# Handing over from one row phase to the next in a two-layer PEER trunk: tokens spread inside the last run, sum read behind the first groups, groups dealt anew

## What is computed

```python
def one_block(xb):                       # 128 tokens
    q = (xb @ w_q).reshape(128, 8, 2, 128)
    s = einsum('tphd,phnd->tphn', q, subkeys)
    s1, i1 = top_k(s[:, :, 0], 16);  s2, i2 = top_k(s[:, :, 1], 16)
    cand = s1[..., :, None] + s2[..., None, :]
    top, pos = top_k(cand, 16)           # 16 experts for each of 8 heads
    g = softmax(top)
    act = gelu(einsum('tped,td->tpe', u[eidx], xb))
    return einsum('tpe,tped->td', g * act, v[eidx])
```

## Time and profile before

| | us |
|---|---|
| runs: median of 3 | 2404.1 (2401.18 to 2404.43) |
| the profiled execution's own time | 2406.2 |
| its span, first to last instruction | 2404.4 |
| mean granted TensorE clock | 0.817 of full |

### The profile page before, as it was taken

One profiled execution on the slowest core, in us unless ns is written; L12 is line 12 of the kernel. 1 busy time (PEld: TensorE's weight loads), 2 busy tenths in 40 slices (PEclk: granted clock), 3 DMA queues, 4 the chain that ended last, 5 costly groups with the idle time before them and its releaser, 6 DMA issues. The chain is left out here.

```text
span 2404.4 us, 28976 instructions
## 1 busy us (share of the span) xinstructions
PE 1595.4 (66%) x9342; PEld 841.6 (35%) x9342; DVE 1567.5 (65%) x4320; ACT 845.8 (35%) x2751; POOL 843.6 (35%) x772
## 2 busy tenths in 40 slices
PE   8986876895965454666764586877577445655554
PEld 6774543563632111333431263545253101200010
DVE  2456787655567778555689558765675897665654
ACT  2324344532323323443333435543232234322232
POOL 0012333432343333243433424343425444444341
PEclk9998897897978777887886898788788677777777
DMA  9978899999899999999999999999999999999996
GB/s 387 408 250 346 326 404 411 397 419 410 345 419 419 420 420 419 396 401 420 414 418 396 419 418 400 371 406 419 417 367 420 422 421 422 421 421 421 422 422 258
DMA packets 156955, 956.48 MB, mean 398 GB/s; under 512 B 19076, under 2 KB 21764, under 8 KB 58500
## 3 DMA queue, kind: packets, MB, share of 16 engines
q0 software_dynamic: 110592, 805.36, 81.2%
q1 hardware_dynamic: 40880, 144.94, 15.6%
q10 hardware_dynamic: 5332, 4.33, 0.7%
HBM read 951.67 MB, written 2.89 MB: 397 GB/s over the span
## 5 line engine op out<-in xcount | busy, mean ns | idle before, releaser
L774 POOL DMA_INDIRECT rows<-in_uv,eidx x768 | 843.4, 1098 | 1516.8 <-PE acc L857 1124.5
L1382 DVE CUSTOM_DVE_ANT_0 rows<-rows,xrep 128x1024 f32<-128x1024 f32 x768 | 911.9, 1222 | 398.2 <-DMA rows<-in_uv,eidx 363.7
L857 PE MATMUL acc<-rows,diag 128*32 128x512 f32 x3072 | 776.8, 751 | 550.3 <-ACT diag L1081 529.1
L857 PEld LDWEIGHTS acc<-rows,diag 128*32 128x32 f32 x3072 | 155.2, 127 | 1072.5 <-ACT diag L1081 701.9
L1081 ACT ACTIVATE act_out<-act_in 128x2 f32<-128x2 f32 x384 | 77.8, 203 | 920.3 <-DVE act_in L1382 886.5
L1081 ACT ACT_TABLE_LOAD x121 | 155.2, 1283 | 232.1 <-DVE act_in L1382 140.7
L792 PE MATMUL bank<-wt,hT 128*128 128x256 f32 x888 | 202.9, 388 | 18.8 <-ACT hT L1081 6.7
L1081 ACT ACTIVATE diag<-small,wv 128x32 f32<-128x32 f32 x768 | 204.9, 314 | 12.5
L792 PEld LDWEIGHTS bank<-wt,hT 128*128 128x128 f32 x888 | 170.3, 194 | 60.2 <-issue 15.7
L1081 ACT ACTIVATE wv<-act_out,gate 128x1 f32<-128x1 f32 x768 | 184.3, 287 | 12.6
L792 PE MATMUL bank<-hT,wt 128*128 128x256 f32 (+1 forms) x896 | 174.0, 356 | 8.4 <-ACT hT L1081 7.9
(11 more groups left out here) (174 smaller groups left out, 1435.0 us busy)
## 6 DMA issues: line engine op xcount, KB each, us to landing
wt<-in_ada_w SPq DMA_DIRECT2D x60, 512.0 KB
wt<-in_peer_w_q SPq DMA_DIRECT2D x48, 512.0 KB
rows<-in_ada_w SPq DMA_DIRECT2D x36, 512.0 KB, 15.2
wt<-in_mlstm_w_in SPq DMA_DIRECT2D x27, 512.0 KB
rows<-in_uv,eidx POOLq DMA_INDIRECT x768
wt<-in_attn_w_qkv SPq DMA_DIRECT2D x24, 512.0 KB
rows<-in_mlstm_w_in SPq DMA_DIRECT2D x21, 512.0 KB, 15.9
rows<-in_peer_w_q SPq DMA_DIRECT2D x16, 512.0 KB, 11.6
```

The costliest lines, as they stand in the source:

```text
L774: nc.gpsimd.indirect_dma_start(out=rows[:, r, :], out_offset=None, in_=A["uv"], in_offset=bass.IndirectOffsetOnAxis(ap=eidx[:, b, slot:slo ...
L857: last = nc.tensor.matmul(acc[c:c + QUAD, h * 512:(h + 1) * 512], diag[:, r, :], rows[:, r, D + h * 512:D + (h + 1) * 512], start=first, s ...
L1382: last = V.tensor_tensor_reduce(out=rows[:, r, 0:D], in0=rows[:, r, 0:D], in1=xrep[:, GS * odd + j, :], scale=1.0, scalar=0.0, op0=ALU.mul ...
```

## The change

1. XR becomes two plan steps, one for each half (slabs 0 and 1, slabs 2 and 3), four PSUM tiles each. Both stand behind GATE, ahead of the phase's last run.
2. On PE half 0 is filled at that place; half 1 is filled behind the last run's groups, before the last owed sums are paid.
3. ACT copies half 0 just ahead of the phase's group 63, when 63 of the 64 groups have had their dot products, and half 1 behind group 63's own work.
4. FIN moves behind the next phase's first groups: 2 in phase two, 1 in phases three and four, 2 in five and six. The load of the cached keys and values (CACHE) goes along with FIN.
5. Phase one's last three groups now follow GATE.
6. DEALS and PATIENCE of phases two, three and four are new. The table shows the groups of the phase that stand ahead of some steps, before and after:

| step | before | after |
|---|---|---|
| phase two: PQ first | 0 | 2 |
| phase two: PQ second, third | 2, 11 | 4, 14 |
| phase three: NORM, NT, AQKV first | 0, 1, 3 | 1, 3, 3 |
| phase three: last PT, PC, PG, GATE | 48, 50, 50, 50 | 47, 47, 49, 49 |
| phase four: NORM, NT, NORM, NT | 0, 3, 6, 6 | 1, 2, 2, 3 |
| phase four: AQKV 1, 2, 3 | 8, 11, 13 | 3, 6, 11 |
| phase four: first and last attention head (AS to AV) | 18 to 21, 37 to 40 | 17 to 19, 39 to 42 |
| phase four: OUT 1, 2 | 44, 50 | 43, 47 |
| phase four: PT, PC, PG; GATE | 58; 61 | 59; 59 |
| phase five: PQ first | 0 | 2 |

```diff
+GORDER = [(0, 0), (0, 1), (0, 2), (1, 0), (1, 1), (1, 2)]
+AHEAD_OF_SUM = 2
...
     def spread(l, b, steps):
 
         steps = list(steps)
-        if (l, b) != (0, 0):
-            yield ("XR", l, b)
+        order = GORDER.index((l, b))
+        following = [("XR", *GORDER[order + 1], half) for half in range(2)] if order + 1 < len(GORDER) else []
+
+        def opening(ahead):
+
+            if ahead:
+                yield ("GROUPS", l, b, 0, ahead, PATIENCE.get((l, b, 0), 2))
+            if order:
+                yield ("FIN", *GORDER[order - 1])
+            if (l, b) == (1, 0):
+                yield ("CACHE",)
+
...
-            if ahead:
-                yield ("GROUPS", l, b, 0, ahead, PATIENCE.get((l, b, 0), 2))
+            yield from opening(ahead)
             for s, n in zip(steps, counts):
                 yield s
+                if s[0] == "GATE":
+                    yield from following
...
-            yield ("FIN", l, b)
             return
         total = sum(cost(s) for s in steps)
-        done = spent = 0
+        done, spent = AHEAD_OF_SUM, 0
+        yield from opening(done)
...
         yield ("GATE", l, b)
+        yield from following
         yield ("GROUPS", l, b, done, GROUPS, 2)
-        yield ("FIN", l, b)
...
             def straight(g0, g1):
                 for g in range(g0, g1):
+                    if g == GROUPS - 1:
+                        before_last()
                     n = base + g
                     body(order, n, g * GS, n % RING, n // RING, g, False, upper(order, g))
...
             if hi == GROUPS:
-                last_ones()
+                behind_last()
...
+            def spread_rows(s):
+
+                first = P * (s[2] == 2)
+                for i in range(QUADS):
+                    t = open_tile(i)
+                    at = first + QUAD * (2 * s[3] + i // 2)
+                    for q in range(4):
+                        for copy in range(QUADS):
+                            last = mm(t[quadrant(copy), q * P:(q + 1) * P], hT[:, 4 * (i % 2) + q, at:at + QUAD], ident, True, True)
+                    last.then_inc(tile_full, 1)
+
+            def close_phase(order):
+
+                if order + 1 < len(GORDER):
+                    begin(PLAN.index(("XR", *GORDER[order + 1], 1)))
+                    spread_rows(("XR", *GORDER[order + 1], 1))
+                settle(0)
...
                 if k == "GROUPS":
-                    run_groups(pe, s, group, looped, lambda: settle(0))
+                    run_groups(pe, s, group, looped, behind_last=lambda: close_phase(GORDER.index(s[1:3])))
...
+            def spread_rows(order, half):
+
+                if order < len(GORDER):
+                    if order:
+                        act.wait_ge(dots, order * GROUPS - 1 + half)
+                        begin(PLAN.index(("XR", *GORDER[order], half)))
+                    for i in range(QUADS):
+                        copy_tile(i, xrep[:, 2 * half + i // 2, 512 * (i % 2):512 * (i % 2) + 512])
...
-                    run_groups(act, s, group)
+                    following = GORDER.index(s[1:3]) + 1
+                    run_groups(act, s, group, before_last=lambda: spread_rows(following, 0), behind_last=lambda: spread_rows(following, 1))
```

More of the change, by code:

```diff
@@ L144, in spread @@
             steps.append(("GATE", l, b))
-            assert len(counts) == len(steps) and ahead + sum(counts) == GROUPS
+            assert len(counts) == len(steps) and ahead + sum(counts) == GROUPS and counts[-1] > 1
             done = ahead
-            if ahead:
-                yield ("GROUPS", l, b, 0, ahead, PATIENCE.get((l, b, 0), 2))
+            yield from opening(ahead)
             for s, n in zip(steps, counts):
                 yield s
+                if s[0] == "GATE":
+                    yield from following
                 if n:
@@ L204, in plan @@
     yield from (("NT", 0, 1, 0), *cell(["MLU"], 0), *cell(["MLU"], 1), ("STATE",))
-    yield from (("PQ", 0, "P", 0), ("PS", 0, "P", 0, 0), ("PQ", 0, "P", 1), ("XR", 0, 0))
+    yield from (("PQ", 0, "P", 0), ("PS", 0, "P", 0, 0), ("PQ", 0, "P", 1), ("XR", 0, 0, 0), ("XR", 0, 0, 1))
     yield from ((k, 0, "P", 0, 0, half) for half in range(2) for k in ("PT", "PC", "PG"))
@@ L218, in plan @@
     yield from spread(0, 2, [*attention("P"), *norm(1, 1, "P"), *choice(1, "P", 0, every, True)])
-    yield ("CACHE",)
     seen = list(attention("S"))
@@ L223, in plan @@
     yield from spread(1, 2, [*choice(1, "S", 1, range(2, QUARTERS), False), ("YOUT", 1)])
+    yield ("FIN", *GORDER[-1])
     yield ("YOUT", 2)
@@ L236, in in_order @@
 def in_order(who):
-    late = {"P": (), "A": ("NT", "MLQK", "MLV", "MLO", "AQKV", "PQ", "OUT", "T2", "PS", "MLB", "MLE", "MLN", "AS", "MR", "XR"),
+    late = {"P": (), "A": ("NT", "MLQK", "MLV", "MLO", "AQKV", "PQ", "OUT", "T2", "PS", "MLB", "MLE", "MLN", "AS", "MR"),
             "D": ("NT", "MLQK", "MLV", "MLO", "MLM", "MLN", "AQKV", "PQ", "OUT", "T2", "PS", "MLB", "MLE", "MLU", "MC", "AS", "AP", "AV")}[who]
@@ L298, in psum_tiles @@
     if k == "XR":
-        return "A" * (2 * QUADS)
+        return "A" * QUADS
     if k == "AT":
@@ L635, in begin @@
                 s = PLAN[i]
-                if s[0] in (*IDLE[who], "GROUPS") or (s[0] == "XR" and who == "A" and s[1:] != (0, 0)) \
+                if s[0] in (*IDLE[who], "GROUPS") or (s[0] == "XR" and who == "A" and s[1:3] != (0, 0)) \
                         or (s[0] == "MC" and (who == "A") != (s[1:3] == (1, 0))) \
@@ L680, in spread_out @@
             def spread_out(order, c):
-                return owner[before[PLAN.index(("XR", *GORDER[order]))][0] + 2 * c + 1][1]
+                return owner[before[PLAN.index(("XR", *GORDER[order], c // 2))][0] + 2 * (c % 2) + 1][1]
             return begin, of, tile, full, by, emptied, next_of, one, noted, spread_out
@@ L707, in upper, with run_groups @@
             return g // (QG // 2) if (order, g // QG) == (0, 0) else g % 2
-        GORDER = [(0, 0), (0, 1), (0, 2), (1, 0), (1, 1), (1, 2)]
-        def run_groups(eng, s, body, looped=lambda n: None, last_ones=lambda: None):
+        def run_groups(eng, s, body, looped=lambda n: None, before_last=lambda: None, behind_last=lambda: None):
             _, l, b, lo, hi, _ = s
@@ L728, in run_groups @@
             straight(lo + 1, g)
-            whole = (hi - g) // UNROLL
+            whole = (hi - g - (hi == GROUPS)) // UNROLL
             if whole >= 2:
@@ L1021, in _ @@
                 elif k == "XR":
[L1022 to L1029, removed]
+                    if s[3] == 0 or s[1:3] == (0, 0):
+                        spread_rows(s)
                 elif k == "AT":
@@ L1270, in _ @@
                 elif k == "XR":
-                    act.wait_ge(dots, GORDER.index(s[1:]) * GROUPS) if s[1:] != (0, 0) else None
-                    for i in range(2 * QUADS):
-                        copy_tile(i, xrep[:, i // 2, 512 * (i % 2):512 * (i % 2) + 512])
+                    if s[1:3] == (0, 0):
+                        spread_rows(0, s[3])
                 elif k == "PG":
```

2 lines of the change are left out of this document (1 added, 1 removed), and 8 rows, old and new, of the table DEALS.

## The result

The changed kernel takes 2390.9 us (median of 6, 2381.8 to 2395.3) against 2402.7 (2401.2 to 2404.4): a ratio of 0.9935, interval 0.9915 to 0.9955. The medians differ by 11.9 us, the ratio stands for 15.6 us (10.8 to 20.4). The forecast was 2388, in the range 2377 to 2402. The experiments ran on three other chips, by all that their times say, and on the one where the changed kernel itself was repeated it won 4.5 us by the medians (3.6 by the ratio, 1.0 to 6.0).

The account below looks back on a forecast made before the run. Transfers were the bound, with time won only where they pause. Handovers 13.4 us plus new deals 3, in all 16, took 2406.2 to 2390; as that execution lay 2.1 above the median, the forecast was 2388, range 2377 to 2402.

Parts of the forecast that it names:

- memory-limit rule: Whole kernel: about 358 GB/s a core from HBM, so filled pauses only slow the rest and nothing is won; chance 0.01.
- The handovers, 13.4 us: Pauses won at phases one to two 4.8 us, two to three 3.2, four to five 5.4; ends 6 and 15.4.
- Rival (b): Handovers win 13.4 us, but full stretches of phases three and four lose 9 to 13: 2400 to 2404 us; chance 0.12.
- old pauses that grow by what the handovers win: Sign of a wrong forecast: existing transfer pauses lengthen by as much as is won between phases.
- Half 0 at nothing: First half of XR on PE ahead of the last run: 4.5 to 5.3 us, hidden by outstanding transfers, so no cost.
- every half 0: By the skill's clock rule, each first half of XR would run at the lower clock, 9 to 10 us.
- 0 to 3 us for the owed sums: Phase one to two: two owed sums behind GATE and half 0 hold two gathers, pausing transfers nothing to 3 us.
- sign of being wrong: A sum delayed over 5 us behind half 0, with the DMA share dropping before the handover.
- DVE's earlier start: New phase's first dot product starts some 1 to 2 us after the last old one; DVE gains 11 to 15 us each.
- Gather 7: Phase one to two: this gather issued near 612 us in place of 624.9, ahead of the 618 when it was due.
- The new deals, 3 us: Groups dealt anew in phases three and four: between winning all 10.9 us and a loss as large, taken as 3.
- The rival of a slower phase four: Three AQKV among phase four's groups 3 to 11 at lower clock: new pause some 30 us, 2418 us; chance 0.07.

Follow-up runs that it names:

- the repeat: The kernel before, run once more without an edit on one of the three other chips: 2383.0 us, ratio 1.0001.
- the repeats: The kernel before and the changed kernel, each run again without an edit on the other chips: 2383.0 us and 2379.6 us.
- XR doubled: The changed kernel with each of XR's small matmuls issued twice: 2387.8 us, ratio 1.0009 to the kernel before.
- the undisturbed repeat: The changed kernel run again without an edit on one of the three other chips: 2379.6 us, ratio 0.9985 to the kernel before.
- before doubled: The kernel before with each of XR's small matmuls issued twice, 512 in place of 256 for each handover: 2419.3 us, ratio 1.0142.

## Why the prediction was right, and where it wasn't

**The bound** was read rightly: what was won in the first profile was, but for some 2 us, pauses filled at an unchanged 421 GB/s. The memory-limit rule of the Trainium skill that the prediction weighed (DMA: Bandwidth & Descriptors, Where 436 GB/s comes from) doesn't fit these runs: the core moved 421 GB/s for 200 us on end, and the closed pauses did shorten the time.

**The handovers, 13.4 us.** On the first chip the three windows came out at 1.00 to 1.02. The single terms: one to two won about 4.3 us of phase two's 6.8 (4.8 put; what is left is 1.1 us behind half 0 and 1.1 us at 640 to 650), two to three 3.2 (3.2), four to five 6.2 (5.4), in all 13.7. The step that was wrong is what stood behind them. I put the 30 us between the gathers down to the order of steps alone. The same order on another chip loses about 2 us in place of 15, nearly all of it at two to three. At one to two and four to five the pauses needed the order and a PE that was late inside XR, by 7.6 and 8.7 us; the earlier trace rows hold it (218 matmuls in a 9.00 us row that begins at 597.36, where GATE ended at 589.9), and so do the tiles "far apart" of the earlier trace rows, which I laid to PE's pauses and the clock. "The whole XR took 9.00 us" was close to the 8.9 us that it takes without the stall, and left the stall out. At two to three XR wasn't late, and why more was lost there than in the repeat is open.

**What was given back.** Rival (b) came true in part, inside a total that came out right. Outside the handover phase three lost 2.5 us before and 8.2 after, so 5.7 of the 13.7 us that the handovers won went again. Its own sign, "old pauses that grow by what the handovers win", stood in the profile. In the repeats it is 3.6 and 7.4. The experiments lay it to the new handover and not to phase three's deals (7.4 to 7.5 with the old ones, 4.9 with the new ones under the old handover). The sum had no term for it.

**Half 0 at nothing.** Its size was right (4.32 us; 9 to 10 us, the whole of it at the lower clock, didn't come). GATE, behind 8.87 us of idling, took 3.75 us in place of 2.05 at a granted clock of 0.50 (1.2 GHz). Half 0 began at that level too, and from about 589.5 on the clock was 1.00 (2.4 GHz). The rule of the Trainium skill (TensorE: Matmul & The Clock Gate, HAM oscillation) held, the lower level followed the pause. What failed is my step from it to "every half 0": GATE stands between the pause and half 0 and took most of the slow stretch. Half 0's cover was nearly right: a pause of 1.1 us. But I took 0 to 3 us for the owed sums from their own order on PE and missed that PE would stand ahead of them waiting for DVE. They came 28 to 35 us behind their dot products, in the sign of being wrong that I had named (over 5 us, with the DMA share dropping: 0.82 in 595 to 600), and with XR doubled the pause there was about 7 us.

**DVE's earlier start.** I gave it 11 to 15 us at each handover and said that nothing there waits for DVE. That is so: it gained 10 to 16 us, FIN ahead takes 4 to 9 of them back, both halves behind 2 to 3, and neither costs anything that can be told.

**Gather 7** was put near 612 and came at 624.6 (625.8 its second half), in an execution that was 6.7 us late, with half 1 stalled; in the undisturbed repeat it came 27 us behind the last dot product, 612 by the first profile's time.

**The new deals, 3 us.** Too small. Phase four's alone are worth 5 to 6 us by the experiments; its losses fell from 6.6 to 0.2, from 9.0 to 3.5 on the first chip. Phase three's win nothing. The rival of a slower phase four (AQKV brought forward) didn't show: there is no pause in that phase's first 60 us in either profile of the changed kernel.

**The number** came out right, 2388 against 2390.9, in part by luck. The handovers, the large term, were sized rightly because profile and result were taken under the same conditions: before read 2402.7 us there again. But the 5.7 us that phase three gave back were left out, and about as much was won in phase four, where the sum had 3 for all deals. A profile from one of the other chips would have shown almost full handovers, and the same steps would then have forecast a few us from the deals.

## What to carry to other kernels

Before pricing a stretch that loses transfers, sum the idle time without a releaser in it; if engines stand still at once there, part of the loss belongs to the execution and may not be there to win on another chip. A window fixed in us from the start misses a pause when an earlier phase ends at another time: place it by the phase's end. Sum the losses of whole phases too, since what one place wins another can give back. A reordering is worth what it hides: here 4.5 us where PE is punctual, 11.9 where XR is 8 us late, 31.6 where it is 12 us late. And when a wait is put ahead of owed work, pay that work first: it was one number here.

## What the runs showed of the chip

- The same program took 2402.7 us in the first comparison, whose chip isn't recorded, and 2384 to 2385 on three chips. In the profiles of the first, PE, ACT and DVE stand still for 51 to 68 us each without a releaser, several at once (589 to 598: PE every two to four matmuls, ACT 6.2 us, DVE 9.25 us). The packets on PE's instruction queue took no longer than elsewhere (1.07 us for 16,384 bytes), and none is recorded from 572 to 601, so nothing ties it to the loading of code of which the next point tells. What causes it stays open.
- Short matmuls seem to outrun their code. PE in XR, before doubled:

```profile
592.09 3.70 PE L792 MATMUL bank<-small,hT 128*32 128x128 f32 x128 [1.47 <-issue]
598.29 5.31 PE L792 MATMUL bank<-small,hT 128*32 128x128 f32 x128 [2.50 <-issue]
604.48 1.95 PE L792 MATMUL bank<-small,hT 128*32 128x128 f32 x62 [0.89 <-issue]
```

  The pauses are exactly 128 matmuls apart, and each begins 0 to 1.5 us behind the start of a packet of 16,384 bytes on an instruction queue (589.56, 595.78, 602.10). 128 matmuls with their weight loads are 256 instructions. The Trainium skill (Runtime: NRT & Kernel Launch, Instruction fetch mechanics) has blocks of 16 KiB or 256 instructions that the sequencer fetches by a queue of its own, at a cost mostly hidden. The size agrees. The cost isn't hidden here, at 29 ns a matmul: 0.9 to 2.5 us each time, 4.9 us in this XR. That the fetch is the cause is read from the times alone, no run tested it. These pauses are part of why doubling XR cost more than its matmuls.
- One kernel's executions spread by more than many a change is worth: before over 15 us in 34 and in 35 runs on two chips, the changed kernel over 13.5 us in six on the first, where before's six lay within 3.2. Part of it is the stretch ahead of the first dot product, 174 to 181 us long in the ten profiles of the experiments with XR as it is, and 179 and 186 us in the first two, with the same order of steps there.
